# A two-layer transformer block in fp32: the GLA's first keys and states, and the splits of the output units, at other places in the order

## The reference, cut to what matters

```
p = h @ w_in                                   # differential attention's q, k, v; GLA's q, k, v, gate, low-rank gates
od = softmax(q1 k1) v - lam * softmax(q2 k2) v # 4 heads, per block of 128 queries
# GLA: 4 heads, chunks of 64 tokens, forward and backward in time
g = cumsum(log gates within the chunk)
att = tril((q * exp(g - g_mid)) @ (k * exp(g_mid - g)).T)
ds  = (k * exp(g_last - g)).T @ v              # per chunk
state = exp(g_last) * state + ds               # from chunk to chunk
og = att @ v + (q * exp(g)) @ state
y = concat(rms(od) * .., rms(og) * silu(gate)) @ w_out
```

## Time and profile before

| | us |
|---|---|
| median of 3 runs | 1870.34 (1867.86 to 1872.07) |
| profiled execution | 1867.63 |
| its span in the trace | 1865.8 |
| TensorE busy | 1772.5 |
| VectorE busy | 1263.3 |
| ScalarE busy | 992.5 |

### The profile page before, as it was taken

The page is one execution under the profiler, slowest core; times in us unless marked ns, Lnnn a source line. Parts: engine busy times, 40 slices in busy tenths (PEclk is TensorE's granted clock), DMA queues, the critical chain, the costliest instruction groups (busy, mean ns, idle before and its releaser), DMA issues.

```text
span 1865.8 us, 26095 instructions
## 1 busy us (share of the span) xinstructions
PE 1772.5 (95%) x10238; PEld 1448.0 (78%) x10238; DVE 1263.3 (68%) x1549; ACT 992.5 (53%) x1327; POOL 53.0 (3%) x40
## 2 busy tenths in 40 slices
PE   6999797999999999999688999999999999999996
PEld 4877576988888887977577888888887777788885
DVE  3336545677677434526557999898976668798987
ACT  4426534622222224517447777777765557676765
POOL 0000000000000000000000150001000000000000
PEclk9999987999999999999887999999999999999998
DMA  8411071244467321311035999898976669898995
GB/s 320 167 46 68 14 250 54 91 181 176 162 251 268 141 107 68 122 68 68 1 114 181 346 384 363 341 365 340 365 268 248 246 229 370 316 373 338 361 362 203
DMA packets 56833, 407.55 MB, mean 218 GB/s; under 512 B 6322, under 2 KB 6450, under 8 KB 7808
## 3 DMA queue, kind: packets, MB, share of 16 engines
q1 hardware_dynamic: 56128, 404.38, 57.7%
q0 software_dynamic: 288, 0.79, 0.1%
q10 hardware_dynamic: 288, 0.63, 0.1%
HBM read 404.73 MB, written 1.05 MB: 217 GB/s over the span
## 4 chain that ended last, share of the span: by engine, by line
PE 88%; DVE 6%; ACT 4%; issue 1%; DMA 1%; SPq 0%; POOL 0%; DVEq 0%; ACTq 0%
PE psum L2134 72%; PE psum L2622 2%; DVE w_lo L1456 1%; PE psum L2712 1%; PE psum L2724 1%; PE psum L2333 1%; PE psum L2677 1%; PE psum L2427 1%; DMA raw<-units 1%; PE psum L2433 1%; PE psum L2160 1%; DVE states L1669 1%; PE psum L2151 1%; PE psum L2355 1%; ACT xn L946 1%
## 5 line engine op out<-in xcount | busy, mean ns | idle before, releaser
L1921 DVE TENSOR_TENSOR w_lo<-raw,w_hi 128x2048 fp32r<-128x2048 f32 x122 | 278.9, 2290 | 62.7 <-ACT w_hi L1285 62.2
L1285 ACT ACTIVATE w_hi<-raw 128x2048 fp32r<-128x2048 f32 x122 | 234.0, 1919 | 111.5 <-PE psum L2134 80.9
L1456 DVE TENSOR_TENSOR w_lo<-raw,w_hi 128x1024 fp32r<-128x1024 f32 x130 | 153.1, 1220 | 163.9 <-ACT w_hi L911 163.5
L2134 PE MATMUL psum<-act_hi,w_hi 128*128 128x512 f32 (+1 forms) x608 | 221.0, 364 | 2.8 <-DVE w_lo L1456 2.8
L2134 PE MATMUL psum<-act_hi,w_lo 128*128 128x512 f32 (+1 forms) x608 | 218.9, 360 | 0.0
L2134 PE MATMUL psum<-act_lo,w_hi 128*128 128x512 f32 (+1 forms) x608 | 218.7, 360 | 0.0
L911 ACT ACTIVATE w_hi<-raw 128x1024 fp32r<-128x1024 f32 x130 | 130.3, 1053 | 161.8 <-DMA raw<-units 87.4
L2134 PE MATMUL psum<-w_hi,xt_hi 128*128 128x512 f32 x528 | 208.8, 396 | 0.0
L1921 DVE TENSOR_TENSOR w_lo<-raw_more,w_hi 128x2048 fp32r<-128x2048 f32 x79 | 180.7, 2290 | 40.3 <-ACT w_hi L1285 39.9
L2134 PE MATMUL psum<-w_hi,xt_lo 128*128 128x512 f32 x528 | 206.7, 391 | 0.0
L2134 PE MATMUL psum<-w_lo,xt_hi 128*128 128x512 f32 x528 | 206.6, 391 | 0.0
(11 more groups left out here) (350 smaller groups left out, 3398.6 us busy)
## 6 DMA issues: line engine op xcount, KB each, us to landing
raw<-units SPq DMA_DIRECT2D x275, 1024.0 KB, 4.9
raw_more<-units SPq DMA_DIRECT2D x107, 1024.0 KB, 5.2
X<-ctx_in SPq DMA_DIRECT2D x1, 1024.0 KB, 8.8
X<-x_in SPq DMA_DIRECT2D x1, 1024.0 KB, 10.8
out<-X SPq DMA_DIRECT2D x2, 512.0 KB, 2.8
const<-const_in ACTq DMA_DIRECT2D x1, 524.0 KB, 7.7
rope<-rope_in POOLq DMA_DIRECT2D x2, 256.0 KB, 5.3
wsm<-wsm_in SPq DMA_DIRECT2D x1, 384.0 KB, 7.8
```

The source lines that it names most:

```text
L1285: act.activation(w_place(m)[0], raw_place(m), ACT.Copy).then_inc(esem("w_high"), 1)
L1456: ins = dve.tensor_tensor(w_lo[:, w_slot(i), part], raw[:, i % RING, part], w_hi[:, w_slot(i), part].bitcast(F32), ALU.subtract)
L1921: dve.tensor_tensor(lo, raw_place(m), hi.bitcast(F32), ALU.subtract).then_inc(esem("w_ready"), 1)
L2134: ins = pe.matmul(dst, lhs(a), rhs(b), start=first and n == 0, stop=last and n == 2)
```

## The change

- The first pair's keys are turned in step n-1 of the attention and its states made in step n, ahead of PT(n-1), on fixed banks (KT on 6 and 7, DS on 0 to 3). ScalarE copies the keys at the end of step n-1, into a part of the split weights' slots (`early_keys`).
- For the second pair, dp 1's differences move to step n of the attention, dp 3's behind the first two scans, and both exponentials on ScalarE behind the attention, ahead of `head_squares`.
- The split of the output units in the GLA: high parts at the items in `HIGH_IN_GLA`, low parts at those in `LOW_IN_GLA`. In layer 0 only unit 0 is split there; unit 1's high part is made by ScalarE ahead of the merge, its low part by VectorE at the start of the out projection.
- In the load order, layer 0's output unit 0 comes ahead of the last two modulation units.

```diff
-    return (start_loads() + stage("in", 0, IN_F + IN_K)[STREAMED:] + [("mod",) + m for m in ATT_MODS[0]]
-            + stage("out", 0, OUT_UNITS) + ffn + stage("down", 0, DOWN_UNITS) + stage("in", 1, IN_F + IN_K)
+    mods, outs = [("mod",) + m for m in ATT_MODS[0]], stage("out", 0, OUT_UNITS)
+    return (start_loads() + stage("in", 0, IN_F + IN_K)[STREAMED:] + mods[:-2] + outs[:1] + mods[-2:] + outs[1:] + ffn + stage("down", 0, DOWN_UNITS) + stage("in", 1, IN_F + IN_K)
...
+def out_unit(l, u):
+    return NUMBER["out", l, u]
-SUBS_IN = {0: {4: 0, 5: 2, 13: 1, 14: 3}, 1: {2: 0, 3: 2, 6: 1, 7: 3}}
-EXPS_IN = {0: {5: 0, 6: 2, 14: 1, 15: 3}, 1: {3: 0, 4: 2, 7: 1, 8: 3}}
+SUBS_IN = {0: {4: 0, 5: 2, 16: 1}, 1: {2: 0, 3: 2, 8: 1}}
+EXPS_IN = {0: {5: 0, 6: 2}, 1: {3: 0, 4: 2}}
 PRODUCTS_IN = {0: {6: 0, 7: 2}, 1: {4: 0, 5: 2}}
 SPLIT_IN = {0: 3, 1: 1}
-OUT_SPLITS = {0: 13, 1: 5}
+HIGH_IN_GLA = {0: {11: 0}, 1: {4: 0, 5: 1}}
+LOW_IN_GLA = {0: {13: 0}, 1: {6: 0, 7: 1}}
...
+            states_of = lambda dps: [("DS", l, dp, half) for dp in dps for half in range(2)]
+            if i == n:
+                out += states_of(PAIR_ORDER[:2])
             if 1 <= i <= n:
                 out.append(("PT", l, i - 1))
             if i >= 2:
                 out.append(("O", l, i - 2))
+            if i == n - 1:
+                out += [("KT", l, dp) for dp in PAIR_ORDER[:2]]
             out += beside(l, i)
-        states_of = lambda dps: [("DS", l, dp, half) for dp in dps for half in range(2)]
-        out += [("KT", l, dp) for dp in PAIR_ORDER[:2]] + states_of(PAIR_ORDER[:2])
...
         banks.update({("K", l) + tile: 6 + k % 2 for k, tile in enumerate(tiles)})
+        for k, dp in enumerate(PAIR_ORDER[:2]):
+            banks["KT", l, dp] = 6 + k
+            banks.update({("DS", l, dp, half): 2 * k + half for half in range(2)})
...
+    early_keys = [at(f"early_keys{l}", A_LO + w_slot_of(in_unit(l, IN_F + 4)) * UNIT, [P, 2, TILES, P]) for l in range(DEPTH)]
...
+    def keys_of(l, dp):
+        return early_keys[l][:, dp // 2, :, :] if dp % 2 == 0 else klT[:, dp, :, :]
...
-                split_upto(mod_unit(l, j) + ahead)
+                if ahead is not None:
+                    split_upto(mod_unit(l, j) + ahead)
...
+                if i == n - 1:
+                    keys_copied(l, PAIR_ORDER[:2])
+
+        def keys_copied(l, dps):
+            for dp in dps:
+                copy_out(("KT", l, dp), keys_of(l, dp).rearrange("p t n -> p (t n)"), bank(("KT", l, dp)))
...
         def gla(l):
-            def keys_copied(dps):
-                for dp in dps:
-                    copy_out(("KT", l, dp), klT[:, dp, :, :].rearrange("p t n -> p (t n)"), bank(("KT", l, dp)))
-
-            keys_copied(PAIR_ORDER[:2])
+            for dp in PAIR_ORDER[2:]:
+                gate_exps(l, dp)
             t0 = token_tiles(l, "out")[0]
             head_squares(l, 0)
             head_squares(l, 1)
             for i, (h, t) in enumerate(gla_items(l)):
-                if i in (OUT_SPLITS[l], OUT_SPLITS[l] + 1):
-                    split_upto(U["out", l] + i - OUT_SPLITS[l])
+                if i in HIGH_IN_GLA[l]:
+                    split_upto(out_unit(l, HIGH_IN_GLA[l][i]))
                 if i == TURNS_AT[l] - 1:
-                    keys_copied(PAIR_ORDER[2:])
+                    keys_copied(l, PAIR_ORDER[2:])
...
                 for key in beside_gla(l, i + 1):
                     if key[0] == "mod":
-                        mod_step(*key, ahead=0)
+                        mod_step(*key, ahead=None)
...
-                split_upto(U["out", l] + u + 2)
+                split_upto(out_unit(l, u + 2))
...
             gates_on_all(l, 0, sides(l))
+            split_upto(out_unit(l, 1))
             merged(l)
...
             scan(l, 0)
             scan(l, 2)
+            gate_differences(l, 3)
             for i, (h, t) in enumerate(gla_items(l)):
-                if i in (OUT_SPLITS[l], OUT_SPLITS[l] + 1):
-                    split_upto(U["out", l] + i - OUT_SPLITS[l])
+                if i in LOW_IN_GLA[l]:
+                    split_upto(out_unit(l, LOW_IN_GLA[l][i]))
...
             for u in range(first):
-                split_upto(U["out", l] + u + 1)
+                split_upto(out_unit(l, u + 1))
                 for t in token_tiles(l, "out"):
                     gated(("mix", l), ("Y", l, u, t), u, D_MODEL // OUT_UNITS)
-            split_upto(U["out", l] + OUT_UNITS - 1)
+            split_upto(out_unit(l, OUT_UNITS - 1))
...
                 for step in fill_steps(l, i):
                     fill_step(l, *step)
+                if i == n:
+                    state_steps(l, PAIR_ORDER[:2])
...
                     ins.then_inc(filled, 1)
+                if i == n - 1:
+                    keys_turned(l, PAIR_ORDER[:2])
                 beside_item(l, i)
 
-        def gla(l):
+        def keys_turned(l, dps):
+
+            for dp in dps:
+                key = ("KT", l, dp)
+                pe.wait_ge(sem(f"gmul{l}"), 4 * PAIR_ORDER.index(dp) + 1)
+                wait_emptied(pe, key)
+                for t in range(TILES):
+                    ins = pe.transpose(bank(key)[:, t * P:(t + 1) * P], factors(l, 2, dp)[:, t * P:(t + 1) * P], ident)
+                ins.then_inc(filled, 1)
...
+        def state_steps(l, dps):
+
             for t in range(TILES):
                 wait_copied(pe, ("K", l, 1, t))
-
...
+            for dp in dps:
+                pair = dp % 2
+                wait_copied(pe, ("KT", l, dp))
+                for half in range(2):
+                    key = ("DS", l, dp, half)
                     wait_emptied(pe, key)
+                    r = slice(half * CHUNK, (half + 1) * CHUNK)
                     for t in range(TILES):
-                        ins = pe.transpose(bank(key)[:, t * P:(t + 1) * P], factors(l, 2, dp)[:, t * P:(t + 1) * P], ident)
+                        for hh in range(2):
+                            ins = pe.matmul(bank(key)[hh * QK:(hh + 1) * QK, t * P:(t + 1) * P],
+                                            keys_of(l, dp)[r, t, hh * QK:(hh + 1) * QK],
+                                            gv[r, t, (2 * pair + hh) * P:(2 * pair + hh + 1) * P], start=True, stop=True)
                     ins.then_inc(filled, 1)
...
-            keys_turned(PAIR_ORDER[:2])
-            state_steps(PAIR_ORDER[:2])
+        def gla(l):
             items = gla_items(l)
             for i in range(len(items) + 1):
                 if i == TURNS_AT[l]:
-                    keys_turned(PAIR_ORDER[2:])
+                    keys_turned(l, PAIR_ORDER[2:])
                 if i == TURNS_AT[l] + 1:
-                    state_steps(PAIR_ORDER[2:])
+                    state_steps(l, PAIR_ORDER[2:])
```

More of the change, by code:

```diff
@@ L497, in release_points @@
         for u in range(OUT_UNITS):
-            at[U["out", l] + u] = ("job", FILL["Y", l, u, TILES - 1])
+            at[out_unit(l, u)] = ("job", FILL["Y", l, u, TILES - 1])
     for j in range(UP_UNITS):
@@ L1112, in attention @@
                 for unit in rows_copied_in(l, i):
-                    mod_step("mod", *unit, ahead=0)
+                    mod_step("mod", *unit, ahead=None)
                 if 1 <= i <= n:
@@ L2361, in gla @@
+        def state_steps(l, dps):
             for t in range(TILES):
                 wait_copied(pe, ("K", l, 1, t))
-            def keys_turned(dps):
-                for dp in dps:
-                    key = ("KT", l, dp)
-                    pe.wait_ge(sem(f"gmul{l}"), 4 * PAIR_ORDER.index(dp) + 1)
+            for dp in dps:
[3 more added lines that the diff above has]
+                    key = ("DS", l, dp, half)
                     wait_emptied(pe, key)
+                    r = slice(half * CHUNK, (half + 1) * CHUNK)
@@ L2371, in keys_turned @@
                     ins.then_inc(filled, 1)
-            def state_steps(dps):
-                for dp in dps:
-                    pair = dp % 2
-                    wait_copied(pe, ("KT", l, dp))
-                    for half in range(2):
-                        key = ("DS", l, dp, half)
-                        wait_emptied(pe, key)
-                        r = slice(half * CHUNK, (half + 1) * CHUNK)
-                        for t in range(TILES):
-                            for hh in range(2):
-                                ins = pe.matmul(bank(key)[hh * QK:(hh + 1) * QK, t * P:(t + 1) * P],
-                                                klT[r, dp, t, hh * QK:(hh + 1) * QK],
-                                                gv[r, t, (2 * pair + hh) * P:(2 * pair + hh + 1) * P], start=True, stop=True)
-                        ins.then_inc(filled, 1)
@@ L2449, in columns @@
             def columns(u, t):
-                key, s = ("Y", l, u, t), unit(U["out", l] + u)
+                key, s = ("Y", l, u, t), unit(out_unit(l, u))
                 wait_emptied(pe, key)
```

## The result

The changed kernel took **1839.33 us** (median of 4 runs, 1837.0 to 1840.74), the kernel before 1869.97 (4 runs, 1867.86 to 1872.07): a ratio of 0.9835, 95% interval 0.9818 to 0.9852. The forecast was 1837.6, range 1827 to 1852. Measured once more, later and unedited, it took 1846.01 (5 runs, 1841.3 to 1849.87) against 1869.79: 0.9869, interval 0.9847 to 0.9891. So it is faster by 24 to 31 us. Its own median moved by 6.7 us between the two sets of runs, while that of the kernel before stayed within 0.2; the experiments explain part of that.

What follows compares the result with a forecast made beforehand. TensorE, busy 95% of the span, bounds the kernel, so only idle or half-clock stretches can give time. Layer 0's 11.1 - 0.3 + 12.5 and layer 1's 9.4 make 32.7: 1867.63 becomes 1834.9, median 2.7 above, 1837.6 us; range 1827 to 1852.

Steps and rivals of the forecast that it cites:

- First OG 7.5 earlier: Layer 0, start: with keys, states and scans moved forward, the first OG starts at 225.85 instead of 233.40.
- After, the longest is 2.2, so I take full clock: Layer 0, start: TensorE's longest idle time becomes 2.2 us, too short to lower the clock, giving 11.1 us.
- The 10.6 at KT: Layer 0, turn of the second pair's keys: it comes 10.6 us earlier, behind OG(2) ending at 235.1.
- The prediction's other value for the start, 5.3: Layer 0, start: if the clock falls, the gain there is 5.3 us instead of 11.1.
- Loads: Layer 0, middle: the last two mods, issued two items ahead, cost 0.3 us in all; far bound 2.9 of queueing.
- Tail of layer 0, 12.5: Layer 0, last items: no waits for Am, full clock, last OG 12.5 us earlier; bounds 10.3 and 13.5.
- Layer 1, 4.3 and 5.1: Layer 1: first OG 4.3 us earlier, tail 5.1 more with one low part still showing, 9.4 in all; bounds 7 and 13.
- rival (c): More gain: full clock in layer 1 up to the second states (3.7) and in the first columns (about 3): 1831; 15%.
- rival (a): Half clock: 5.8 lost at the start, 1.9 by an exposed high part, 2 in the tail, 9.7 in sum: 1847.3; 17%.
- (b): Moved work shows: late exponentials, late mod loads and unit 1's exposed high part cost 14 us: 1851.6; 6%.
- (d): Slower: half clock lasts from the attention's end past item 12 to the columns: 1871 or more; 3%.
- (e): The waits stay, because the same Am then waits for another releaser: no change; 2%.

Runs made afterwards that it cites:

- only_splits: The kernel before with only the change's load order and split places; keys, states and the second pair's factors as before: 1849.32 us (0.989).
- fill_layer0: The changed kernel plus ten matmuls with unused results on TensorE ahead of layer 0's first modx: 1836.51 us (0.9804).
- same_item: The changed kernel with layer 0's unit 0 high part at item 13, the item of its low part, instead of item 11: 1856.16 us (0.9921).
- old_order: The changed kernel with the old load order and layer 0's unit 0 high part at item 12 instead of 11: 1849.26 us (0.9879).
- fill_layer1: The changed kernel plus fourteen matmuls with unused results on TensorE ahead of layer 1's first OG: 1839.71 us (0.983).
- row_first: The changed kernel with layer 0's dp 3 exponentials on ScalarE behind the first mod row's copy, the squares behind the next two rows' copies: 1838.51 us (0.9825).
- l1_high_in_7: The changed kernel with layer 1's unit 1 high part at item 7 and its low part at the out projection's start: 1841.36 us (0.9829).
- combined: The changed kernel with the edits of row_and_high7 plus fill_layer1's 14 matmuls with unused results: 1830.01 us (0.9784).
- row_and_high7: The changed kernel with the edits of row_first and l1_high_in_7 together: 1831.48 us (0.9791).

## Why the prediction was right, and where it wasn't

The time came out 1.7 above the forecast, and 8.4 above it in the second set, still in the range. The mechanism holds, with its larger terms. One step took the wrong side, and the closeness of the first number is in part luck: in the profiles the gain was 29.1 (and 26.3 in the second) for the 32.7 forecast. The stages that the change touches gave 29.4 in the first profile, and all else -0.3. The forecast put the median 2.7 above the profiled execution, as before; it came 0.8 above it, which gave 1.9 back.

- **First OG 7.5 earlier**: 6.5. Two terms were too small. The state matmuls began 114.5 behind R0 and not 114.05, since they waited for the copied keys, and the scans 1.13 behind them (223.11 to 224.24) and not 0.65. The trace of before had 1.14 for the latter (226.27 to the scan's first copy at 227.41).
- **"After, the longest is 2.2, so I take full clock"**: this step failed. The idle time was nearly as computed (2.36, with the copy of the row as its releaser), and the clock fell behind it in every profile that has it. The prediction's own sign of being wrong, half clock in items 1 to 4, was there. Length alone doesn't decide: the trace of before had shown 1.00 through 2.34, and only_splits has 1.00 through 2.62. The 10.6 at KT became 7.7 in the first profile and 4.7 in the usual one (141.6 less 136.9). Of what is missing 1.0 is the first OG's; half clock alone is 1.6 and 4.6, by fill_layer0. The prediction's other value for the start, 5.3, is the nearer one in the usual case. Here the Trainium skill, "TensorE: Matmul & The Clock Gate", section "A second HAM failure mode: psum-queue depth-cycling", had spoken against me, and the traces agree with it in that the clock swings among groups of matmuls with idle times between them (0.50 in 232 to 240 of the second profile). They don't bear out frequent short idle times as the cause here, since filling the one long idle time was enough.
- **Loads**: 0.3 taken, 0.41 measured, and 0.26 to 0.74 in the other profiles but two; 2.65 where the load took longer (same_item), inside the far bound.
- **Tail of layer 0, 12.5**: from KT on the table has 12.7; less the turn's own 0.9, and with the load's 0.4 put back, 12.2. There is no wait for Am, all is at 1.00, and unit 1's high part ends as the first `hf` is due (286.41 against 286.52), a cover of 0.1: by the chain of waits VectorE's gated norm ends last there, not the high. What the experiments add is how brittle that is. Where the clock is at half, the same high part is on the path for its 2.0, in same_item and in old_order.
- **Layer 1, 4.3 and 5.1**: 3.8 and 5.1. The start has 106.2 from R1 to the first OG, then 102.4, and 0.75 of the 3.8 was not foreseen: the attention's first eight score matmuls take 1.99 and not 2.74 in all eleven profiles with the early states, at granted clock 1.00 either way, and 2.74 in the kernel before and in only_splits. Why is open. So what was meant gave 3.05 for 4.3. The form of the tail was exact, one low part in item 7 behind the root. The half clock that I left in was there, and is worth 3.3 (fill_layer1).
- **Not foreseen as sure** (a part of rival (c)): the first columns at full clock, 1.75 in the first profile and 0.3 in the second, and 1.5 between there and R1; against them the start of the kernel, 4.5 lost. These are of the size of the spread between two sets of runs.

What rival (a) named, half clock in the first items, is what happens most times. Its number, 1847.3, is near the second median, 1846.0, but not for its reasons: it carried 2 in the tail and 1.9 of exposed high part with it, and in the second profile the tail still gave 12.4 and nothing was exposed. (b), (d) and (e) fell: no moved work shows in the middle, TensorE is at 1.00 from the items behind the turn to the last one, and each half gives its own gain.

Open: what in the second set of the changed kernel's runs made the other four slower than the profiled one (granted clock over the span 0.973 to 0.975 for 0.977; only one was profiled), and why the same idle time takes the clock for one item in one execution and for two in others.

## What to carry to other kernels

When a wait is taken away, look at which wait takes its place on TensorE and at what its price is in clock, not only in idle time: 2.4 us of idling cost 4.6 more in the matmuls behind it in most profiles. Put the step that TensorE asks for first in front of its engine's queue, ahead of work that is wanted later. And split the profile at landmarks before the change and behind it: two medians of one kernel lay 6.7 apart here, while layer 1 from R1 to the last OG copy agreed to 0.5 us in the six profiles where its code is the same (131.8 to 132.3) and showed gains of 3 that the medians hid. Longer stretches spread more: from the last OG copy to R1 the two profiles of the changed kernel have 506.9 and 508.4.

## What the runs showed of the hardware

- The granted clock fell behind idle times of TensorE of 2.35 and 2.36 us in seven profiles of seven, and once each behind 2.65 (same_item) and 2.76 (old_order). It stayed at 1.00 through one of 2.34 in the kernel before and one of 2.62 in only_splits, the same wait for a load as the 2.65. Behind 1.89 us, ahead of layer 0's turns of `od` and `og`, it fell in six profiles (the changed kernel, twice, row_first, fill_layer0, l1_high_in_7, combined) and stayed in three (only_splits, fill_layer1, row_and_high7). Behind 2.35 and 2.36 it came back after one item of the same work, after two, or past the turn of the keys.
- The same first 50 us ran at 1.00 or partly near half in 30 to 50 (0.71, 0.78). R0 came 4.5 us apart in these two profiles, and between 104.0 and 109.4 in all 13.
- A load of 1 MB, the one for mod 18, landed in 5.0 to 5.5 us in most profiles and in 7.4 in only_splits and same_item, with the same order of loads. With a lead of 4.88 that is a wait of 0.3 to 0.7 or of 2.6.
